# An encoder trunk with routed experts: the order of small steps changed at the head norms, the router and the last rows

## The reference, cut to what matters

```python
for i in range(DEPTH):                      # DEPTH = 2, 256 tokens, D_MODEL = 1024
    h = rms_norm(x, g_mix[i])
    proj = h @ w_in[i]
    ...                                     # two mixers, each with a norm per head
    ya = hgrn2_mixer(qa, fa, ia, ga, lb_all[i], hgrn_norm[i])   # rms_norm over heads of 128
    yb = swa_mixer(qb, kb, vb, q_norm[i], k_norm[i], sinks[i])  # rms_norm of q and k, heads of 64
    x = x + merged @ w_o[i]
    h2 = rms_norm(x, g_ffn[i])
    if i % 2 == 0:
        x = x + swiglu(h2, w_dense_gate[j], w_dense_up[j], w_dense_down[j])
    else:
        x = x + moe_swiglu(h2, w_router[j], w_moe_gate[j], w_moe_up[j], w_moe_down[j])
    gate_p = sigmoid(rms_norm(x, g_ple[i]) @ w_ple_gate[i])
    x = x + gate_p * (p[i] @ w_ple_up[i])

def moe_swiglu(h, w_router, wg, wu, wd):    # top 2 of 8 experts
    logits = t @ w_router
    top_vals, top_idx = lax.top_k(logits, TOP_K)
    w = softmax(top_vals)
    gates = sum(one_hot(top_idx, 8) * w, axis=1)
    ...                                     # acc + gate * swiglu(t, wg, wu, wd) over the experts
```

## Time and profile before

| | |
|---|---|
| median of 3 runs | 1672.43 us (1668.36 to 1673.43) |
| the profiled execution, time | 1672.0 us |
| its span | 1670.2 us |
| PE busy | 1640.0 us, 98% |
| DVE busy | 1299.6 us, 78% |
| ACT busy | 1095.1 us, 66% |
| POOL busy | 92.5 us, 6% |
| mean granted PE clock | 0.994 of full speed |

### The profile page before, as it was taken

The page is one execution under the profiler, slowest core; times in us unless marked ns, Lnnn a source line. Parts: engine busy times, 40 slices in busy tenths (PEclk is TensorE's granted clock), DMA queues, the critical chain, the costliest instruction groups (busy, mean ns, idle before and its releaser), DMA issues.

```text
span 1670.2 us, 21541 instructions
## 1 busy us (share of the span) xinstructions
PE 1640.0 (98%) x8191; PEld 1349.0 (81%) x8191; DVE 1299.6 (78%) x1082; ACT 1095.1 (66%) x901; POOL 92.5 (6%) x73
## 2 busy tenths in 40 slices
PE   7999999999999999999999999999999999999998
PEld 6878888888888888788888888888888888888885
DVE  6786754445567776898898888888988888888885
ACT  5556544343555655677877778778778778778773
POOL 1200000000002001000000000000000000000100
PEclk9999999999999999999999999999999999999999
DMA  9434465555453444999999999999999999999990
GB/s 317 170 125 153 153 202 199 177 187 192 164 195 125 152 152 179 325 383 359 381 392 359 383 388 342 392 394 345 394 395 342 395 393 343 395 393 348 393 393 26
DMA packets 201824, 479.98 MB, mean 287 GB/s; under 512 B 8816, under 2 KB 11440, under 8 KB 201776
## 3 DMA queue, kind: packets, MB, share of 16 engines
q1 hardware_dynamic: 198224, 466.20, 76.5%
q0 software_dynamic: 3552, 13.11, 2.8%
HBM read 470.89 MB, written 8.39 MB: 287 GB/s over the span
## 4 chain that ended last, share of the span: by engine, by line
PE 93%; DVE 3%; POOL 1%; issue 1%; ACT 1%; DMA 0%; SPq 0%; DVEq 0%; ACTq 0%
PE ps L1416 28%; PE ps L1418 28%; PE ps L1417 28%; PE ps L1428 2%; PE ps L1818 1%; DVE w_lo L852 1%; PE ps L1425 1%; PE ps L1423 1%; PE ps L1424 1%; POOL head_meansq L497 1%; PE ps L1431 1%; POOL head_rstd L499 0%; PE ps L1850 0%; PE ps L1714 0%; ACT normed L635 0%
## 5 line engine op out<-in xcount | busy, mean ns | idle before, releaser
L852 DVE TENSOR_TENSOR w_lo<-raw,w_hi 128x2048 fp32r<-128x2048 f32 x442 | 1008.0, 2289 | 227.7 <-ACT w_hi L562 225.1
L562 ACT ACTIVATE w_hi<-raw 128x2048 fp32r<-128x2048 f32 x442 | 846.6, 1918 | 343.9 <-PE ps L1418 331.5
L1416 PE MATMUL ps<-w_hi,hT_hi 128*128 128x512 f32 (+1 forms) x1544 | 609.7, 395 | 5.3 <-DVE w_lo L852 3.5
L1418 PE MATMUL ps<-w_hi,hT_lo 128*128 128x512 f32 (+1 forms) x1544 | 599.8, 388 | 0.0
L1417 PE MATMUL ps<-w_lo,hT_hi 128*128 128x512 f32 (+1 forms) x1544 | 599.2, 388 | 0.0
L1416 PEld LDWEIGHTS ps<-w_hi,hT_hi 128*128 128x128 f32 x1544 | 290.9, 188 | 70.6 <-DVE w_lo L852 8.8
L1418 PEld LDWEIGHTS ps<-w_hi,hT_lo 128*128 128x128 f32 x1544 | 290.6, 188 | 61.2
L1417 PEld LDWEIGHTS ps<-w_lo,hT_hi 128*128 128x128 f32 x1544 | 291.1, 189 | 56.1
L1416 PE MATMUL ps<-w_hi,inner_hi 128*128 128x512 f32 x592 | 234.6, 396 | 0.0
L1418 PE MATMUL ps<-w_hi,inner_lo 128*128 128x512 f32 x592 | 231.2, 391 | 0.0
L1417 PE MATMUL ps<-w_lo,inner_hi 128*128 128x512 f32 x592 | 231.0, 390 | 0.0
(11 more groups left out here) (251 smaller groups left out, 857.6 us busy)
## 6 DMA issues: line engine op xcount, KB each, us to landing
raw<-in_w_moe_gate SPq DMA_DIRECT2D x112, 1024.0 KB, 7.6
raw<-in_w_moe_up SPq DMA_DIRECT2D x112, 1024.0 KB, 7.9
raw<-in_w_moe_down SPq DMA_DIRECT2D x112, 1024.0 KB, 7.9
raw<-in_w_in SPq DMA_DIRECT2D x38, 1024.0 KB, 5.9
raw<-in_w_dense_gate SPq DMA_DIRECT2D x14, 1024.0 KB, 5.1
raw<-in_w_dense_up SPq DMA_DIRECT2D x14, 1024.0 KB, 5.1
raw<-in_w_dense_down SPq DMA_DIRECT2D x14, 1024.0 KB, 4.9
raw<-in_w_o SPq DMA_DIRECT2D x8, 1024.0 KB, 4.9
```

The costliest lines, as they stand in the source:

```text
L562: nc.scalar.activation(w_hi[:, n % SLOTS, :], raw[:, n % RAW_SLOTS, :], ACT.Copy).then_inc(high_ready, 1)
L852: nc.vector.tensor_tensor(w_lo[:, n % SLOTS, :], raw[:, n % RAW_SLOTS, :], w_hi[:, n % SLOTS, :].bitcast(F32), ALU.subtract).then_inc(low_ ...
L1416: nc.tensor.matmul(o, x_parts[0][x_cols], parts[0], start=first, stop=False)
L1418: return nc.tensor.matmul(o, x_parts[1][x_cols], parts[0], start=False, stop=last)
```

## The change

- Each head norm's mean plus epsilon is made on DVE, right behind the sum (`head_means`); POOL keeps the power alone.
- The router product is turned round: the router columns are loaded as weights and 256 tokens move, two matmuls per k. The result (16 x 256, both parts of the router) is copied to `logit_parts`, and two small matmuls with `add_parts` turn it back and add the parts. The first of them stand behind the first piece of `ple_up_tile(0)`.
- `gain_x(1)` stands behind `chosen` on DVE.
- PE's counts are made by column halves of 64.
- The item count comes ahead of the gate weights. The first part of `extras` and the read of the count move ahead of the gate weights too, and PE's first slot table waits for `gates_ready`.
- The spreading matrices are made in each item's step 3, on DVE, and no longer after the loop; `slot_last` is gone.
- After the loop PE spreads in the order of `PIECES`, transposes the left half of `x` ahead of the last piece, and the right half inside the first unit of the gate product. ACT and DVE make the left half of `hT` before the right half.

```diff
             def heads_rstd(n, heads):
 
                 pool.wait_ge(head_sums, n + 1)
-                link(nc.gpsimd.tensor_scalar(head_meansq[:, 0:heads], head_sumsq[:, 0:heads], 1.0 / width, EPS,
-                                             ALU.mult, ALU.add))
                 nc.gpsimd.tensor_tensor(head_rstd[:, 0:heads], head_meansq[:, 0:heads], minus_half[:, 0:heads],
                                         ALU.pow).then_inc(head_rstds, 1)
...
+            def head_means(heads, width, squares):
+
+                link(nc.vector.reduce_sum(head_sumsq[:, 0:heads], squares, AX_X))
+                nc.vector.tensor_scalar(head_meansq[:, 0:heads], head_sumsq[:, 0:heads], 1.0 / width, EPS,
+                                        ALU.mult, ALU.add).then_inc(head_sums, 1)
...
             def route():
                 dve.wait_ge(logits_done, 1)
-                for t in range(TILES):
-                    last = nc.vector.tensor_copy(logits[:, t, :], banks(GATE + t)[:, 0:EXPERTS])
-                link(last)
-                for t in range(TILES):
-                    last = nc.vector.tensor_tensor(logits[:, t, :], banks(GATE + t)[:, EXPERTS:2 * EXPERTS], logits[:, t, :], ALU.add)
-                link(last)
+                nc.vector.tensor_copy(logit_parts[:, :], banks(GATE)[0:2 * EXPERTS, 0:SEQ]).then_inc(logits_copied, 1)
+                dve.wait_ge(logits_turned, 1)
+                link(nc.vector.tensor_copy(logits[:, :, :], banks(UP)[:, 0:TILES * EXPERTS].rearrange("p (t e) -> p t e", t=TILES)))
...
+                gain_x(1)
...
                         if s == 2:
...
+                        if s == 3:
+                            nc.vector.tensor_scalar(spread[:, 0:P], column[:, :], slot_now[:, 1:2], None, ALU.is_equal)
+                            nc.vector.tensor_scalar(spread[:, P:2 * P], column[:, :], slot_now[:, 2:3], None,
+                                                    ALU.is_equal).then_inc(spread_ready, 1)
...
-                nc.vector.tensor_scalar(spread[:, 0:P], column[:, :], slot_last[:, 1:2], None, ALU.is_equal)
-                nc.vector.tensor_scalar(spread[:, P:2 * P], column[:, :], slot_last[:, 2:3], None, ALU.is_equal).then_inc(spread_ready, 1)
                 dve.wait_ge(x_summed, 16)
-                for piece in range(4):
+                for piece, (tile, half) in enumerate(PIECES):
+                    if piece == 3:
+                        norm_low(5, PLE_GAIN + KD, range(0, 4))
                     dve.wait_ge(item_combined, piece + 1)
...
-                        mm(banks(GATE + t)[:, 0:2 * EXPERTS], hT[0][columns(k, t)], router_parts[:, k, :, :], k == 0, False)
-                        last = mm(banks(GATE + t)[:, 0:EXPERTS], hT[1][columns(k, t)], router_parts[:, k, 0, :], False, k == KD - 1)
+                    mm(banks(GATE)[0:2 * EXPERTS, 0:SEQ], router_parts[:, k, :, :].rearrange("p n e -> p (n e)"), hT[0][:, k, :],
+                       k == 0, False)
+                    last = mm(banks(GATE)[0:EXPERTS, 0:SEQ], router_parts[:, k, 0, :], hT[1][:, k, :], False, k == KD - 1)
...
+                ple_up_tile(0, [(0, 0)])
+                pe.wait_ge(logits_copied, 1)
+                for t in range(TILES):
+                    last = mm(banks(UP)[:, t * EXPERTS:(t + 1) * EXPERTS], logit_parts[:, t * P:(t + 1) * P], add_parts[:, :], True, True)
+                last.then_inc(logits_turned, 1)
+                ple_up_tile(0, [(0, 1), (1, 0), (1, 1)])
...
-                pe.wait_ge(spread_ready, 1)
-                for piece in range(4):
-                    pe.wait_ge(item_y_ready, count * 2 + 2 - (piece < 2))
-                    spread_piece(piece, 2 * (1 - piece // 2) + piece % 2)
+                pe.wait_ge(spread_ready, count)
+                for piece, (t, half) in enumerate(PIECES):
+                    pe.wait_ge(item_y_ready, count * 2 + 1 + half)
+                    if piece == 3:
+                        pe.wait_ge(gatheredT_ready, count * 2 + 2)
+                        flip_summed_x(0)
+                    spread_piece(t, half)
+                pe.wait_ge(item_added, 3)
```

More of the change, by code:

```diff
@@ L1235, in route, with extra_places @@
                                              top[:, :].unsqueeze(2).to_broadcast([P, TILES, EXPERTS]), ALU.mult))
[L1236 to L1241 removed]
+                nc.vector.tensor_copy(item_gate_w[:, :, 0:EXPERTS], gate_w[:, :, :]).then_inc(gates_ready, 1)
+                extra_gates()
+                return count
+            def extra_places():
                 pa1 = pair_a[:, 0, :, :]
@@ L1773, in gather_first @@
+                for own in CHUNKS:
+                    mm(counts[own], ones[:, own], chosen[:, 0, :], True, False)
+                for own in CHUNKS:
+                    last = mm(counts[own], ones[:, own], chosen[:, 1, :], False, True)
+                last.then_inc(places_done, 1)
             def gather_first():
```

132 lines of the change are left out of this document (67 added, 65 removed).

## The result

The changed kernel takes 1657.37 us (median of 4 runs, 1654.84 to 1657.48), against 1671.86 for the kernel before (4 runs). The ratio estimated from all these runs is 0.9918, 95% interval 0.990 to 0.9936. Timed again later, it took 1657.14 (6 runs, 1655.11 to 1658.22) beside 1671.03 (11 runs, 1666.51 to 1675.03): 0.9919, interval 0.9903 to 0.9934. So it is some 14 us faster.

The account below looks back on a forecast made before the run. PE was taken as busy throughout the expert loop, leaving only its stops and the half-clock stretches behind them to win. 0 - 3.1 + 0 - 3.4 = -6.5 us on 1672.0 gave 1665.5 us, range 1659.0 to 1670.0.

Parts of the forecast that it names:

- Head norms: Both mixers: POOL's power waits behind DVE's splits as the mean did, PE's 1.98 us stop stays; 0 us.
- The first rival: Mixers: POOL's power gets its ports ahead of DVE's splits; 6.4 us in both, 1659.1 us; chance 0.12.
- Routing: Routing to the loop: the third unit's `w_lo` is ready earlier, PE's stop falls from 3.4 to 1.2 us; -3.1 us.
- 0.85 + 1.36 + 0.9: Routing: gathered rows 0.85 us earlier, 1.36 gone from DVE's tail, 0.9 for the count read; `w_lo` 3.1 us earlier.
- the walk along DVE's list: Routing: DVE's operations timed in turn up to the third unit's `w_lo`, ready 3.1 us earlier.
- the forecast's two cases: Routing: PE keeps full clock, -3.1 us, or falls to half clock as before, 1.8 us.
- between these I take that it stays: Loop's entry: the half-clock stretch from 677.70, costing 2.5 us, was taken to remain behind the shorter stop.
- My lower bound (-5.6): Routing: the forecast -3.1 us with the 2.5 us of half clock at the loop's entry gone too.
- Expert loop: Loop step 3: about 0.5 us more DVE work in each of 8 items is covered; 0 us, bound 4 us.
- After the loop: Behind the last item: spreading starts without the 2.67 us wait, eight transposes move into the gate product; -3.4 us.
- half clock gone: Loop's entry: the slow stretch vanishes altogether; 2.5 us more, -9.0 in all, 1663.0 us; chance 0.12.

Follow-up runs that it names:

- no_mean: The kernel before with POOL's mean left out and the power taken of the bare sum, DVE's list untouched; POOL's power took 10.13 us.
- scalar_behind: The kernel before plus, on DVE behind the head sum, a wait for it and an instruction with unused result; first mixer 70.66 us against 73.16.

## Why the prediction was wrong

**Head norms: 0 forecast, 5.8 measured. This step failed, and it is most of the error.** The mechanism was read rightly: POOL is held off by DVE's run of operations with two SBUF operands, whatever POOL's instruction is. no_mean gave the power the 10 us that the prediction named. What failed is the sentence that DVE "writes the mean 0.2 us behind the sum and at once starts the same two splits", as if its run were then the same. `head_means` has a wait for the sum in it (`link`), and that wait opens the ends of DVE's instructions to POOL. The first rival ("POOL is not locked out", 0.12) has the right size, 6.4 for both mixers against 5.8, and the wrong reason: POOL doesn't come first, it comes 2 us later, at the end of a split. The row that would have warned was there, in the first group on POOL: the power at 24.60 took 2.68 us and not 0.70, so it was set free at 26.58, at the end of one split, though DVE's next instruction reads two operands from SBUF as well. Ahead of those splits DVE's list has a `link`, a wait for its own last result, at line 886:

```profile
21.97 0.17 DVE L886 TENSOR_SCALAR lb_rest<-lb 128x8 f32<-128x8 f32 x1
22.17 4.54 DVE L852 TENSOR_TENSOR w_lo<-raw,w_hi 128x2048 fp32r<-128x2048 f32 x2
```

That fits the kernels above. I read the row only for the lock, and not for where it let go. The 0.6 us that the same rival put down for half clock in the mixers are not there (73.15 at full clock, 73.16 with it).

By the Trainium skill (SBUF — State Buffer, two separate sides), whichever comes first holds the shared ports for the whole instruction and the other fully blocks. For DVE against POOL the trace agrees: nothing gets in inside a split. For POOL against DVE it does not, and the measurement decides: once let in at 76.10, the power computed until 79.64 while DVE's second split and level operations of two SBUF operands ran their usual 2.28 and 0.68 us. Without a wait five ends of DVE's instructions passed by before POOL was served; with one it was the first.

**Routing: 3.1 forecast, 6.2 measured.** To DVE's first split in the loop 3.7 were gained, where 0.85 + 1.36 + 0.9 = 3.1 were forecast: DVE is at the first gathered rows 1.39 us earlier for the 0.85, and what follows is 2.28 shorter for the 2.26. PE's stop is 1.10 for the 1.2 forecast. So the walk along DVE's list held. The 3.7 hold the full clock behind the router product, as the forecast's 3.1 did: old lists at full clock there need 23.6 to 23.7 us to that split, so 1.3 of them are clock (the forecast's two cases differ by 1.3 too). The term that was mis-sized is the clock at the loop's entry: "between these I take that it stays". It went, and DVE's first split to the end of the first item takes 109.87 us and not 112.42: 2.55, as the bound of 2.5 had it. Compare scalar_behind: the old list at full clock takes 222.27, so the new order is worth 2.4 of the 6.2, and 3.8 are clock. My lower bound (-5.6) held full clock at both places; it missed the 6.2 by the 0.6 that the walk had been short.

**Expert loop: 0 forecast, 0.1 measured.** The two added operations in step 3 are hidden.

**After the loop: 3.4 forecast, 3.5 to 3.8 measured.** PE stopped 0.81 us ahead of the transposes, for the forecast's 0.9. Here too a part is clock: the three old lists that happened to keep it full need 42.5 us, the nine that did not 43.8 to 45.5, and the new order, at full clock in all six profiles that have it, 40.4 to 40.8. So the order is worth about 2 us and the clock the rest. The forecast's 3.4 took full clock here and has 1.6 for it, so its agreement is not luck.

**The range.** Its lower end stood on the first rival alone. With two rivals true at once (not locked out, half clock gone: 1665.5 - 6.4 - 2.5 = 1656.6) the sum is within 1 us of the result; that it is so near is luck in part, since the first rival's way for POOL was another. Rivals that don't exclude each other have to be added for the range.

## What to carry to other kernels

A wait on an engine is not only a cost: where GpSimd waits for ports behind a run of VectorE operations with two SBUF operands, one wait in that run at which VectorE stands empty (here for its own last result; its next instruction starts some 0.1 us later for it; waits that are met already do nothing) gave 5.1 us over two layers, with nothing moved. So when an edit touches the list of an engine that locks another out, ask whether it also adds or takes away a wait in it. And when stops are shortened, count the stretch at half clock behind each as its own term, with both outcomes, and let the outcomes of all of them into the range together.

## What the runs showed of the hardware that I had not expected

- With one wait of DVE's in the run, POOL got in at the next end of an instruction (held 0.4 to 2.1 us); without, it was held 6.6 us over six instructions. POOL's power then runs beside DVE's two-operand operations, which take 0.03 to 0.04 us longer once.
- PE's half clock behind a stop comes or stays away in the same list. Of the 18 profiles, by place:

| place, and PE's stop there | profiles with half clock behind it |
|---|---|
| first mixer, 1.97 to 1.98 us | 2 of 6 |
| second mixer, 1.96 to 1.97 us | 4 of 6 |
| behind the old router product, no stop | 7 of 11 |
| behind the turned router product | 0 of 7 |
| loop's entry, 3.4 us | 10 of 11 |
| loop's entry, 1.1 to 1.5 us | 1 of 7 |
| after the loop, 2.6 to 2.7 us | 9 of 12 |
| after the loop, 0.8 us | 0 of 6 |

  So one profile of a kernel shows one draw of each. The kernel before ran from 1666.4 to 1675.0 us, the changed one from 1654.8 to 1658.2. Part of that narrower spread is, by these columns, that fewer places are left where the clock can fall.
- The first products of a program ran at half their speed in 6 of 18 profiles; in the changed kernel's the granted clock reads 1.00 there all the same:

```profile
14.90:18.70 3.80, 3.80 (x9) 1.00 1.04 384
```
